# FFN up-projection: partial sums completed in PSUM, normalisation moved to the down evictions, weight sums on VectorE, first blocks in eight products

## The reference, cut to what matters

```python
def rmsnorm(x, g):
    xf = x.astype(jnp.float32)
    y = xf * lax.rsqrt(jnp.mean(xf * xf, axis=-1, keepdims=True) + RMS_EPS)
    return (y * g.astype(jnp.float32)).astype(x.dtype)

def swiglu(h, w1, w3, w2):
    return (jax.nn.silu(h @ w1) * (h @ w3)) @ w2
...
    h = rmsnorm(x, w['norm_ffn1'])
    x = x + 0.5 * swiglu(h, w['ffn1_w1'], w['ffn1_w3'], w['ffn1_w2'])
...
    h = rmsnorm(x, w['norm_ffn2'])
    x = x + 0.5 * swiglu(h, w['ffn2_w1'], w['ffn2_w3'], w['ffn2_w2'])
    gate = jax.nn.sigmoid(rmsnorm(x, w['norm_ple']) @ w['w_ple_gate'])
    x = x + gate * (ple.astype(x.dtype) @ w['w_ple'])
```

## Time and profile before

| what | value |
|---|---|
| median of 3 runs | 2723.18 us (2722.01 to 2725.67) |
| the profiled execution's own time | 2725.64 us |
| its span, first to last instruction | 2723.8 us |
| granted TensorE clock, mean | 0.985 |
| busy: PE, PEld | 2603.0 us (96%), 2447.8 us (90%) |
| busy: DVE, ACT, POOL | 1933.8 us (71%), 1185.9 us (44%), 542.2 us (20%) |
| DMA | 304.38 MB, mean 112 GB/s |

### The profile page before, as it was taken

The page is one execution under the profiler, slowest core; times in us unless marked ns, Lnnn a source line. Parts: engine busy times, 40 slices in busy tenths (PEclk is TensorE's granted clock), DMA queues, the critical chain, the costliest instruction groups (busy, mean ns, idle before and its releaser), DMA issues.

```text
span 2723.8 us, 54467 instructions
## 1 busy us (share of the span) xinstructions
PE 2603.0 (96%) x22804; PEld 2447.8 (90%) x22804; DVE 1933.8 (71%) x2315; ACT 1185.9 (44%) x1674; POOL 542.2 (20%) x326
## 2 busy tenths in 40 slices
PE   5999999999999899999979999999999998999997
PEld 5999999976699899999969999999757998999997
DVE  7999437665676799953689993476566668999436
ACT  5555323423663555532355552244236535555323
POOL 1432200332000143320024331003220002432300
PEclk9999999999999999999989999999999999999999
DMA  3232332268422123332212232322783222233231
GB/s 106 95 101 99 96 120 99 81 225 285 147 84 88 63 93 100 101 111 83 92 64 93 93 104 97 120 96 94 257 277 107 91 80 69 95 99 106 96 99 64
DMA packets 142109, 304.38 MB, mean 112 GB/s; under 512 B 14946, under 2 KB 25186, under 8 KB 141410
## 3 DMA queue, kind: packets, MB, share of 16 engines
q1 hardware_dynamic: 141922, 301.79, 33.5%
HBM read 290.30 MB, written 11.44 MB: 111 GB/s over the span
## 4 chain that ended last, share of the span: by engine, by line
PE 72%; DVE 14%; DVEq 10%; ACT 2%; issue 2%; ACTq 0%; POOLq 0%
PE ps L645 33%; PE ps L736 14%; PE ps L693 14%; DVEq L1919 4%; DVEq L1925 3%; DVE ta L1882 3%; DVE ULa L1882 2%; DVE tb L1882 2%; PE ps L909 2%; DVEq L1929 2%; DVE G L1882 1%; PE ps L1001 1%; DVE weven L1882 1%; DVE wodd L1882 1%; PE ps L1020 1%
## 5 line engine op out<-in xcount | busy, mean ns | idle before, releaser
L645 PE MATMUL ps<-Gh,ring 128*128 128x260 f32 x2816 | 453.7, 283 | 0.0
L736 PE MATMUL ps<-HA,UHa 128*128 128x260 f32 x2112 | 391.7, 286 | 59.9 <-DVE HA L1354 38.0
L736 PEld LDWEIGHTS ps<-HA,UHa 128*128 128x128 f32 x2112 | 330.2, 191 | 63.1 <-DVE HA L1354 30.5
L645 PEld LDWEIGHTS ps<-Gh,ring 128*128 128x128 f32 x2816 | 386.0, 188 | 0.0
L693 PE MATMUL ps<-Hh,ring 128*128 128x260 f32 x2048 | 342.3, 286 | 0.1
L736 PE MATMUL ps<-HA,ULa 128*128 128x260 f32 x1056 | 301.0, 285 | 0.0
L693 PEld LDWEIGHTS ps<-Hh,ring 128*128 128x128 f32 x2048 | 285.2, 188 | 4.3 <-issue 2.7
L1802 POOL TENSOR_TENSOR weven<-weven,weven 128x512 f32<-128x512 f32 x88 | 136.0, 1546 | 749.8 <-DMA weven<-in_ffn_up 742.7
L645 PE MATMUL ps<-Gl,ring 128*128 128x260 f32 x1408 | 282.6, 282 | 0.0
L736 PE MATMUL ps<-HB,UHb 128*128 128x260 f32 x1408 | 270.3, 289 | 7.1 <-DVE ULb L1882 7.1
L1882 DVE TENSOR_TENSOR ring<-rawd,ring 128x1408 fp32r<-128x1408 f32 x64 | 110.3, 1724 | 190.0 <-ACT ring L1371 190.0
(11 more groups left out here) (322 smaller groups left out, 5617.3 us busy)
## 6 DMA issues: line engine op xcount, KB each, us to landing
weven<-in_ffn_up SPq DMA_DIRECT2D x88, 512.0 KB, 4.7
wodd<-in_ffn_up SPq DMA_DIRECT2D x88, 512.0 KB, 4.9
rawd<-in_ffn_down SPq DMA_DIRECT2D x128, 352.0 KB, 3.4
kb<-in_cache_k SPq DMA_DIRECT2D x128, 256.0 KB, 4.0
kb<-in_cache_v SPq DMA_DIRECT2D x128, 256.0 KB, 4.0
raw<-in_w_in SPq DMA_DIRECT2D x56, 512.0 KB, 4.7
raw<-in_w_gate SPq DMA_DIRECT2D x32, 512.0 KB, 4.6
raw<-in_w_ab SPq DMA_DIRECT2D x16, 512.0 KB, 4.3
```

The lines of the kernel that those rows point to most:

```text
L645: last = nc.tensor.matmul(ps[:, bank + 2 * m + c, 0:HT], w, x[:, k0 + k, c * HT:(c + 1) * HT], start=starts and k == 0 and n == 0, stop=st ...
L736: last = nc.tensor.matmul(ps[:, 4 * p + BANK[f], 0:HT], a[:, w], x[:, i, :], start=f in (0, 1, 2, 5) and i == 0 and t == 0, stop=i == 3 an ...
```

## The change

- **Evictions.** Three of the four copies of ACT now end where PE adds to them: f = 0 is copied from bank 2 to bank 1 in PSUM, f = 4 from bank 2 to bank 0, and PE goes on adding in banks 1, 0 and 2. u is then complete in PSUM, and `up_u` is one multiplication by `R`. v is one addition, is not multiplied by `R` and has its sign turned; each down eviction (8 per FFN) multiplies by `R` (tile `dt`) and adds with factor -0.5. PE's waits for the copies change: f = 2 waits for the copy of f = 0, f = 4 for those of 0, 1 and 2, f = 6 for that of f = 4.
- **Weight sums.** All four are on DVE, for block n+2 in iteration n. POOL keeps `gate_low`.
- **First blocks.** Block 0 of each FFN, and blocks 1 and 2 of (0,0), are plain: eight products, 96 matmuls (`up_plain`), from activations without sums (`raw_act`, `raw_dve`). The sums of activations (`form_*`) follow between them. Even norms use `accu` and banks 4 and 5. In (0,0), PE waits for the root before block 1; elsewhere ACT does, before the copy of f = 0.

```diff
+        def plain(L, hid):
+
+            return 1 if L or hid else 3
...
-                if f in (3, 4, 6):
-                    pe.wait_ge(up_copy, 4 * n + (4 * g + {3: 1, 4: 2, 6: 3}[f]))
...
+                    pe.wait_ge(up_copy, 4 * n + (4 * s + 1))
                 elif f == 4:
                     pe.wait_ge(split_done, n + (L * NB + nb + FREE + 1))
+                    pe.wait_ge(up_copy, 4 * n + (4 * s + 3))
+                elif f == 6:
+                    pe.wait_ge(up_copy, 4 * n + (4 * s + 4))
...
+                up_plain(L, nb, ub, hid, 0, PWh[hid], PWl[hid], raw_part)
                 norm_sum(L, nj)
+                if np > 1:
+                    pe.wait_ge(rt_ready, L * NORMS + (nj + 1))
+                    up_plain(L, nb, ub, hid, 1, UHa, ULa)
+                    up_plain(L, nb, ub, hid, 2, PWh[hid], PWl[hid])
+                up_block(L, nb, ub, hid, np, 1, all_forms)
...
+            V.tensor_tensor(s[:, 0:2, :], GX[:, 1:3, :], GX[:, 0:1, :].broadcast_to([P, 2, HT]), ALU.subtract)
+            dve.drain()
+            V.scalar_tensor_tensor(out=s[:, 2, :], in0=s[:, 1, :], scalar=-1.0, in1=GX[:, 1, :], op0=ALU.mult, op1=ALU.subtract)
+            dve.drain()
+            V.scalar_tensor_tensor(out=s[:, 3, :], in0=GX[:, 3, :], scalar=-1.0, in1=s[:, 2, :], op0=ALU.mult, op1=ALU.subtract
...
+                    if n >= np:
                         up_high(L, nb, hid, n, 2)
+                        if n == 1:
+                            act.wait_ge(rt_ready, L * NORMS + (nj + 1))
+                        up_out(L, hid, n, 0)
                     if n:
                         up_silu(L, hid, n - 1)
+                    if n >= np:
+                        up_out(L, hid, n, 1)
+                    if n == 0 and np == 1:
+                        form_scaled(act, L, nj, hid, 3)
+                    next_high(n + 1, 0)
...
+                    if n >= np:
+                        up_out(L, hid, n, 2)
                     if 0 < n <= GE:
                         gate_high(L, hid, n - 1)
+                    next_high(n + 1, 1)
...
+                    if n >= np:
+                        up_out(L, hid, n, 4)
                 act.wait_ge(up_form, 6 * up_first(L, hid) + 6 * KF - 2)
                 down_high(L, nb + KF, 0)
-                up_out(L, nb, nj, hid, KF - 1, 6)
...
+            def up_sums(L, nb, hid, n):
+
+                w, v = WF[n % 2]
+                dve.wait_ge(raw_ready[n % 2], (L * NB + nb + n) // 2 * 32 + 32)
+                TT(w[:, 1, :], w[:, 0, :], v[:, 2, :], ALU.add).then_inc(up_sum, 1)
+                dve.drain()
+                TT(w[:, 3, :], w[:, 1, :], v[:, 0, :], ALU.add).then_inc(up_sum, 1)
+                TT(v[:, 2, :], v[:, 2, :], v[:, 0, :], ALU.add)
+                dve.drain()
+                TT(v[:, 1, :], w[:, 3, :], w[:, 2, :], ALU.add).then_inc(up_sum, 1)
...
-                u = halves(ta[:, n % 2, :])
-                TT(u, pair(4 * (n % 2)), u, ALU.add)
-                dve.drain()
-                TT(ta[:, n % 2, :], ta[:, n % 2, :], R[:, :], ALU.mult).then_inc(ta_ready, 1)
...
+                TT(halves(ta[:, n % 2, :]), pair(4 * (n % 2)), halves(R[:, :]), ALU.mult).then_inc(ta_ready, 1)
...
                     if n:
                         up_u(L, nb, hid, n - 1)
+                        up_v(L, hid, n - 1)
+                    if n >= np:
+                        up_low(L, nb, hid, n, 2)
                     if n:
                         up_g(L, hid, n - 1)
+                    next_low(n + 1, 0)
...
+                    next_low(n + 1, 1)
+                    if np <= n + 2 < KF:
+                        up_sums(L, nb, hid, n + 2)
...
+                        TT(halves(dt[:, :]), pair(2 * (s % 4)), halves(R[:, :]), ALU.mult)
+                        dve.drain()
+                        V.scalar_tensor_tensor(out=X[:, m, :], in0=dt[:, :], scalar=-0.5, in1=X[:, m, :],
```

More of the change, by code:

```diff
@@ L442, in up_first, with formed @@
             return (2 * L + hid) * KF
+        def plain(L, hid):
+            return 1 if L or hid else 3
+        def formed(L, hid, n):
+            return sum(KF - plain(*f) for f in ((0, 0), (0, 1), (1, 0))[:2 * L + hid]) + n - plain(L, hid)
         def half_t(c):
@@ L710, in first_pair, with up_waits @@
                 block8(L, n + 1, u + 1, 1, nj)
[L712 to L719, removed]
+            WH = [UHa[:, 0, :], UHa[:, 1, :], UHa[:, 3, :], UHa[:, 2, :], UHb[:, 2, :], UHb[:, 0, :], UHb[:, 1, :]]
+            WL = [ULa[:, 0, :], ULa[:, 1, :], ULa[:, 3, :], ULa[:, 2, :], ULb[:, 2, :], ULb[:, 0, :], ULb[:, 1, :]]
+            XH = [XR[:, 0], HS[:, 1], HS[:, 2], XR[:, 2], HS[:, 0], HS[:, 3], XR[:, 1]]
+            XL = [XR[:, 3], HS[:, 5], HS[:, 6], XR[:, 5], HS[:, 4], HS[:, 7], XR[:, 4]]
+            BANK = (2, 3, 2, 1, 2, 3, 0)
+            def up_waits(L, nb, ub, hid, n, f):
+                g, s = up_first(L, hid), formed(L, hid, 0)
                 if f == 0:
@@ L742, in up_block @@
-            def up_block(L, nb, ub, nj, hid, n, p):
+                last.then_inc(block_done if f == 6 else up_form, 1)
+            def up_block(L, nb, ub, hid, n, p, before=None):
                 for f in range(7):
-                    up_waits(L, nb, ub, nj, hid, n, p, f)
+                    up_waits(L, nb, ub, hid, n, f)
+                    if before and f == 1:
+                        before()
                     up_product(p, f)
[L747 to L760, removed]
-                norm_sum(L, nj)
[L762 to L766, removed]
@@ L1817, in ffn @@
                 for n in range(KF):
-                    up_sums(L, nb, hid, n)
-                    if 2 <= n < GE + 2:
-                        gate_low(L, hid, n - 2)
-                for n in range(GE, KF):
                     gate_low(L, hid, n)
@@ L1928, in up_g, with up_v @@
+            def up_v(L, hid, n):
+                v = halves(tb[:, n % 2, :])
+                if n < plain(L, hid):
+                    V.tensor_scalar(v, pair(4 * (n % 2) + 2), -1.0, None, ALU.mult).then_inc(evac, 1)
+                else:
+                    dve.wait_ge(up_copy, 4 * formed(L, hid, n) + 4)
+                    TT(v, pair(4 * (n % 2) + 2), v, ALU.add).then_inc(evac, 1)
             def up_g(L, hid, n):
@@ L1937, in ffn, with next_low @@
             def ffn(L, nb, ub, nj, hid):
+                np = plain(L, hid)
+                def next_low(n, g):
+                    if n < np:
+                        plain_low(L, nb, hid, n, g)
+                    elif n < KF:
+                        up_low(L, nb, hid, n, g)
+                if np == 1:
+                    form_sums(dve, L, hid, 3)
+                    up_sums(L, nb, hid, 1)
                 for n in range(KF):
@@ L1983, in to_u @@
                 last.then_inc(evac, 1)
[L1986 to L1993 removed]
+            V.memset(accu[:, :], 0.0)
+            dve.drain()
+            for m in range(KD):
+                raw_dve(dve, 0, 0, 0, m)
+                if m == 1:
+                    for q in range(2):
+                        plain_low(0, 0, 0, 0, q)
+                square_dve(dve, 0, 0, m)
             dve.wait_ge(loads, 16)
```

347 lines of the change are left out of this document (187 added, 160 removed).

## The result

| what | before | after |
|---|---|---|
| median | 2723.18 us (2720.83 to 2725.77, 5 runs) | 2734.91 us (2732.62 to 2737.43, 5 runs) |
| the profiled execution's own time, its span | 2725.64, 2723.8 us | 2732.62, 2730.8 us |
| granted TensorE clock, mean | 0.985 | 0.991 |

The ratio after to before is 1.0042, with a 95% interval of 1.0027 to 1.0057: the kernel became slower, by 0.42%. Predicted were 2727.5 us and a range of 2708 to 2752. The time lies in the range and in the forecast's own range; it is 7.4 us over the forecast. The forecast's sum, +4.3 us, was within the 0.2% that a measurement can tell, the result is not. The forecast had no firm direction: its chances were 0.34 for faster, 0.3 for no difference and 0.36 for slower.

What follows compares the result with a forecast made beforehand. Before, a DVE stretched by POOL's lock bounded early up blocks and PE late ones; after, a DVE load loop. Starts (+3.1, +1.2, -3.6, +1.2) and down stages (+2.4) sum to +4.3: median 2723.2 to 2727.5 us, range 2708 to 2752.

Steps and rivals of the forecast that it cites:

- The closed loop: Up stages: DVE's sums wait for a load released by its own last `ULb`; 11.1 us per turn, 74 turns.
- ACT's copies: Up stages: ACT's copies, 0.39 us each, lie off the loop's path; the three before product 4 end about with `ULb`.
- The loop that doesn't bind: Rival, up stages: PE's pace everywhere, 70 us less, 2658 us; chance 0.1.
- The lock moving into the loop: Rival, up stages: late `gate_low` delays DVE's sums, 0.8 us in 10 blocks of 4 FFNs, +30, 2757 us; chance 0.14.
- The landing seen sooner: Rival, up stages: loop near 10.9 us, no effect in late blocks, -15, 2713 us; chance 0.14.
- turn, 74 times: Up stages: time from the end of one `ULb` to the next, 11.1 us in each of 74 turns.
- e in (0,0): Start of (0,0): first formed `ULb` ends at 72.8 us; the up stage ends 3.1 us later than before.
- e in (0,1), (1,0), (1,1), the last on the first's start: Starts of the other FFNs: first formed `ULb` ends at 948.0, 1392.3, 948.0; stages change by +1.2, -3.6, +1.2 us.
- down start, each: Start of each down stage: ACT's copy of f = 4 stands ahead of `down_high`, 0.6 us late, four times, +2.4.
- down eviction in FFN 1, each: Down stages: the eviction's extra pass of 0.77 us is covered, cost 0; uncovered it would be 4 x 0.8.
- the next stage needs the last chunk 10 us after it starts: Ends of down stages: reason given for charging 0 for the longer eviction.
- the reciprocal of (0,1): Sign, start of (0,1): DVE's reciprocal starts 2 us after the root is ready.

Runs made afterwards that it cites:

- experiment 3: Kernel after, with sums of block n+1 behind g on DVE and ACT's copy of f = 2 ahead of the next block's first high part: 2651.25 us.
- experiment 4: Kernel after, but for n > 3 SP loads only 128 of 512 weight columns, order unchanged: 2662.95 us, one run.
- experiment 9: Kernel after, but SP loads the half of the weights that `ULa` reads as soon as `ULa` of block n is written: 2663.54 us.
- experiment 2: Kernel after, with only ACT's copy of f = 2 moved ahead of the next block's first high part: 2738.18 us, one run.
- experiment 1: Kernel after, with only DVE's order changed, sums of block n+1 behind g in iteration n: 2717.52 us.
- experiment 8: On top of experiment 3, the first two weight sums of each formed block made on POOL again: 2657.84 us.
- experiment 6: On top of experiment 3, ACT's high part of the first down product ahead of its copy of f = 4 of the last block: 2646.64 us.
- experiment 7: Experiment 6 plus, in (0,0), root and reciprocal ahead of the first sums of activations: 2646.91 us.

## Why the prediction was right, and where its size was off

**The closed loop: right.** The prediction added 5.43 + 2.70 + 1.24 + 1.745 = 11.1 us per turn and 74 turns. Measured: 11.149 over 74 turns, early and late blocks alike but for the five late landings, against 11.27 in early and 10.16 in late blocks before. Experiments 3, 4 and 9 take the transfer off the loop in three ways (DVE's order, fewer bytes, an earlier issue of half), and each brings PE's pace back. The clock is no part of it: over nearly all of the four up stages (80 to 263, 962 to 1163, 1410 to 1610 and 2311 to 2510 us) it is 1.00. It did fall at a place that the prediction doesn't mention, right behind PE's idle stretches of 4.0 to 5.7 us before the first formed block of the last three FFNs. In (0,1) and (1,0) of the kernel after (us, busy times, granted clock, DMA):

```profile
950.00:956.00 6.00, 5.24 (x24) 5.24 (x25) 4.27 (x4) 2.56 (x5) 1.53 (x1) 0.51 0.56 177
1398.00:1404.00 6.00, 5.99 (x27) 5.99 (x28) 3.56 (x3) 1.96 (x3) 1.54 (x1) 0.50 0.56 177
```

In the second window PE gets through 27 matmuls in the time of 50 at 0.12 us. So it is late for the next blocks, and has no wait in the first two turns of (0,1) and the first of (1,0); but DVE, whose queue sets the turn, doesn't wait for PE there, and the loop loses nothing. The Trainium skill (DMA: Bandwidth & Descriptors, "Rules for kernel authors"), issue early and wait late, agrees with these runs: issuing half early brings the mean turn from 11.15 to 10.06 (experiment 9), and waiting late to 10.03 (experiment 3).

**ACT's copies: right, with less room than it seemed.** PE has no wait behind one in the kernel after, and experiment 2 finds no gain in moving one. But with the load off the loop, the order on ACT's queue caps the turn at 10.77 (experiment 1), 0.4 us below the loop. Each order alone is worth 17 us or nothing, both together 84.

**Rivals.** The loop that doesn't bind (2658): refuted, 54.0 us of waits behind `ULb` in the turns. Its number is close to what the kernel reaches once the order is changed, so PE's pace was a true limit that this order doesn't reach; it is 10.05, not the 10.16 of the prediction. The lock moving into the loop (2757): `gate_low` does stretch one `ULa` to 1.74, ahead of the landing, and early turns are no longer than late ones apart from the late landings. The landing seen sooner (2713): 11.149, no.

**The terms that were mis-sized**, in us (e is the end of the first formed `ULb`, in the clock of the trace before):

| term | predicted | measured |
|---|---|---|
| turn, 74 times | 11.1 | 11.149: +3.6 |
| e in (0,0) | 72.8 | 74.78: +2.0 |
| e in (0,1), (1,0), (1,1), the last on the first's start | 948.0, 1392.3, 948.0 | 948.3, 1392.0, 948.2 |
| down start, each | +0.6 | +0.55 at the most |
| down eviction in FFN 1, each | 0 | +0.84 |
| mixers | 0 | -3.2, -2.9 in this pair of profiles |

The turns are longer by two small errors that are not in the landing. Its mean over the 74 is 5.41 us (5.43 predicted): most landings are shorter than that, 5.35 in the mean, and the five late landings make up for it. The rest of a turn is 5.74 and not 5.69, above all since four sums take 2.76 us (2.70 predicted), and the sum of 11.115 was rounded down to 11.1: -1.3 for the landing, +3.8 for the rest and +1.1 for the rounding give the +3.6. The start of (0,0) is where the sum is most off: it had 1.22 for the second `ULa` before the first formed block; it took 2.00, as `gate_low` ran from 66.23 to 68.05 beside it, and the rest of the 2.0 was lost ahead of it on DVE's queue, in hand-overs with ACT. In the down stage "the next stage needs the last chunk 10 us after it starts" is true after FFN 0 only; after FFN 1 the gate product needs the same chunk, and the uncovered 0.8 that the prediction itself named applies, for two of the four. What the terms add up to: 4.3 as predicted, 3.6 for the turns, 2.2 for e, 1.7 for the down evictions of FFN 1 and 0.2 for those of FFN 0, together 12.0. The profiles show 7.0 and the mixers' 6.1 on top, 13.1; the remaining 1.1 us lies behind the last turn of the four stages and isn't broken down further. So the prediction's place, +4.3 and no difference that can be measured, was off by small terms of mostly one sign, the largest of them the turns and the start of (0,0), whose +2.0 is outside the +-1.5 that the prediction allowed a start. The mechanism was right, but an error of 8 us in the sum was enough to leave the direction open.

The signs that it named were there: the reciprocal of (0,1) starts at 944.27 with the root ready at 941.7, 2.6 us (2 predicted); PE starts at 19.86 (19.5), the root of (0,0) comes at 42.4 (42.5), PE waits 8.3 us for it (10). DVE is idle 1.0 to 1.5 us behind the DMA in early turns, 2.1 to 2.5 in late ones (1 and 2), leaving the late landings aside. PE's wait in a turn is 0.76 us (1.0), its waits for `ring` are 0.55 at most (0.6). One step was off without an effect: block 0 of (0,0) ends at 34 and not at 31, as its first matmuls are 0.22 us apart and not 0.12; the root came later than that in any case.

**Left open.** Why five landings take up to 1.4 us more than the others. Three of them, the first behind e in the last three FFNs, fall into the stretches of low clock, but the two others of (1,0), 6.03 and 5.88, have a clock of 1.00; in the five late landings most of the data comes in the usual time and a small rest is late, and no experiment separates the cause. Which part of the change brings early blocks from 11.27 down to PE's pace once the order is turned: it isn't the place of the sums (experiment 8), and no run puts back the evictions of the up stage. And whether the plain blocks are worth their 12 matmuls each: no kernel ran without them.

## What to carry to other kernels

When a wait for a transfer moves to another engine, look for what releases that transfer. If the release stands behind the wait on the same engine's queue, landing time and work add up to a loop that no busy share shows; add its starts up and compare with the pace of the engine that should bind. Breaking it by order means working on the transfer that was released a turn ago, and then the next queue in line (here ACT's copy behind a high part) must be turned as well: turning ACT's queue alone gave nothing, DVE's alone 17 us, both 84.

## What the runs showed of the hardware

- The granted clock fell to 0.91 to 0.95 in the same stretches of the mixer in some executions and stayed at 1.00 in others, with the same code and within 0.2 us of the same place (experiments 6 and 7). The time differs by some 3 us per mixer.
- The granted clock also fell to 0.50 right behind idle stretches of PE of 4.0 to 5.7 us, and stayed there for some 3 to 7 us while PE was busy again. It cost nothing here, where DVE set the pace.
- A copy of 128x260 on ACT from one PSUM bank to another takes 0.37 us, from PSUM to SBUF 0.37 to 0.39. The prediction had left up to 0.69 open for it.
- DVE's `ULa` is stretched by POOL's `gate_low` in early blocks, from 1.22 to 1.74 us. The `ULa` that starts at 110.58 ends at 112.32, which is 1.08 us after the end of POOL's instruction at 111.24:

```profile
109.68 1.56 POOL L1875 TENSOR_TENSOR Gl<-G,Gh 128x520 fp32r<-128x520 f32 x1 [9.58 <-ACT Gh L1426]
```

  That is the contention that the Trainium skill describes (SBUF — State Buffer, "Who interferes with whom"); here it costs nothing, since it lies beside a transfer.
- A transfer of two times 512 KB, issued by SP at the end of an instruction of DVE, was seen by DVE 5.1 to 5.7 us after that end in 69 of 74 turns and 5.85 to 6.81 in the others; one of 512 KB (experiment 9), or two of 128 KB (experiment 4), within 4.1 us in steady turns. How much sooner isn't shown, since DVE was busy until then.
